# Four rows of expert weights outside the ring instead of two, other pieces for the first and last experts, three transfers and one block of copies moved

## The chip, the core and the metric

The kernel runs on one core of a Trainium2 chip. The metric is the device time of one execution in microseconds (us). Five engines work side by side, each with a queue of its own: TensorE (PE, with weight loads PEld), VectorE (DVE), ScalarE (ACT), GpSimd (POOL) and SyncE (SP), which here issues nearly all DMA transfers. Engines wait for one another through semaphores.

## The reference

```python
def reference(x, ...):                      # x: (1, 256, 1024) float32
    h = x
    p = rmsnorm(h, norm_mix_g) @ w_in       # 8480 columns
    y_conv = short_conv_mixer(...)          # width-3 convolution
    y_rwkv = rwkv7_time_mix(...)            # 16 heads of 64, recurrent state
    h = h + (gate_conv * y_conv + gate_rwkv * y_rwkv) @ w_out
    hn = rmsnorm(h, norm_ffn_g)
    h = h + moe_ffn(hn, router_w, router_b, exp_w1, exp_b1, exp_w2, exp_b2)
    return rmsnorm(h, norm_final_g)

# moe_ffn: 32 experts, 4 of them for each token; for an expert
#   u = x_e @ w1[e] + b1[e]                 # w1[e]: 1024 x 2048 float32, 8 MB
#   y = clamped_swiglu(u) @ w2[e] + b2[e]   # w2[e]: 1024 x 1024 float32, 4 MB
```

## The kernel before

The program has a mixer stage (up to about 386 us in the trace) and an expert stage. The mixer stage takes `w_in` through three buffers in "chunks"; chunk 0 holds the LoRA columns, chunk 1 the first half of the key columns. It ends with the product with `w_out`, the routing and the ranks of the tokens.

**The expert stage** takes all 32 experts one after another. An expert's weights are 12 *rows* of 128 x 2048 float32 (1 MiB each): rows 0 to 7 are `w1`, rows 8 to 11 are `w2`. They lie in `ring`, which has 16 slots of one row. SP issues the loads in the order of use; a load covers 1, 2 or 4 rows, a *piece*. `PARTS` lists the pieces of each kind of expert as (first row, rows), `AT` the slot of its row 0. Before a piece, SP waits in `used` until PE has finished the rows whose slots the piece takes (`w1_used`, `w2_used`). PE waits once for each piece, at the piece's first row, for its whole landing (`row_landed`). So DMA can be at most 16 rows ahead of PE, and the last piece of a slot group decides.

For expert 1, two of its rows (4 and 5) do not lie in the ring but in buffers that are free by then: `side` and the work array `i_SW` (`SIDE`, `load_side`, L496). They let SP load 18 rows before PE has used any: 12 of expert 0, rows 0 to 3 of expert 1, and these two.

PE's work for one expert (`expert`): eight `w1` rows of 8 matmuls each (L1131, `first_rows`); then `between`: the gates of the expert before (`combine`, L1105), the gather of the next expert's tokens (`gather`, L1095), the turn of the activations (L1159), the gates' turn (L1166), the bias of the second product (L1173); then four `w2` rows (L1145, `second_rows`), and the next expert's first bias (L1074). DVE and ACT do SwiGLU meanwhile. The last two experts are interleaved in `last_two` (L1202), with the pieces `w1_30`, `w1_31`, `w2_30`, `w2_31`. `combine` waits for `y_ready`, DVE's copy of the second product out of PSUM (`take_second`, L2173). In the last expert `last_sum` releases the final norm.

**Biases.** `exp_b1` and `exp_b2` are loaded three times each by SP into 96 partitions (L477, L479), behind chunk 2 of `w_in`, and split into three bf16 parts by POOL (L1607 to L1633). POOL first waits for the constants (`const_rest`). At the same time, DVE works on the decays: a scan (L1732) and what follows it, up to the reciprocal (L1747) for which PE waits before L687.

**Final norm.** ACT loads its weights, `gfin`, between its last cast before the expert loop and that loop (L1538). DVE seeds the four PSUM banks of the output with the residual (L2150) after the gates of expert 0, as its last work before the expert loop.

## Time and profile before

| what | value |
| --- | --- |
| median of 3 runs | 1306.29 us (1305.19 to 1309.45) |
| the profiled execution, its own time | 1311.27 us |
| its span, first to last instruction | 1308.7 us |
| PE busy | 1222.7 us, 93% of the span |
| mean granted TensorE clock | 0.981 |
| DMA read | 448.16 MB |
| mean DMA rate over the span | 343 GB/s, about 430 GB/s in the expert stage |
| chain that ended last | PE 67%, DMA 28%, DVE 3% |

The span lies 2.6 us below the profiled execution's own time, and that execution is 5.0 us above the median of the runs: a difference of two versions is worked out on the profiled execution and then taken from the median. In the rows of a timeline the bracket at the end tells how long the engine stood idle ahead of that row, and what released it. All times in rows are us from the start of the span.

### The profile page before, as it was taken

To read this page: it belongs to the slowest core of one execution; us is meant where nothing else is said; L and a number is where in the kernel's file an instruction comes from. 1 tells how busy PE (TensorE), PEld (TensorE's weight loads), DVE (VectorE), ACT (ScalarE), POOL (GpSimd) and SP (SyncE) were. 2 spreads that over 40 slices of the span, in tenths; PEclk is the share of its full clock that TensorE was granted. 3 is DMA by queue.
4 is the path that set the end of the run, shared out by engine and by line. 5 is a ranking of instruction groups with operands and counts; after the bars stand their busy time and mean duration, and the time that the engine had idled before them with its cause. 6 is when DMAs were issued, how large, how long until landed. Compare 5 with 4: busy or idle time off the path is not lost.

```text
span 1308.7 us, 23654 instructions
## 1 busy us (share of the span) xinstructions
PE 1222.7 (93%) x10432; PEld 635.2 (49%) x10433; DVE 310.3 (24%) x615; ACT 213.7 (16%) x345; POOL 57.5 (4%) x32
## 2 busy tenths in 40 slices
PE   8999999999999999998898999899889988998997
PEld 6878888888653343333333333334333333343332
DVE  2473433233151221112111111112111111121112
ACT  4532221311041110001110000011000000011101
POOL 0800120000020000000000000000000000000000
PEclk9999999999989999999999999999999999999999
DMA  9621232246969899999999999999999999999996
GB/s 291 204 72 58 95 104 67 67 131 211 422 260 421 359 433 426 427 430 436 423 433 431 433 423 429 430 431 434 429 428 426 429 431 431 427 432 433 424 431 257
DMA packets 56811, 450.13 MB, mean 344 GB/s; under 512 B 6000, under 2 KB 23920, under 8 KB 35664
## 3 DMA queue, kind: packets, MB, share of 16 engines
q1 hardware_dynamic: 53664, 446.85, 82.6%
q10 hardware_dynamic: 3088, 2.37, 0.6%
q8 instruction: 51, 0.84, 0.3%
q14 instruction: 8, 0.07, 0.0%
HBM read 448.16 MB, written 1.05 MB: 343 GB/s over the span
## 4 chain that ended last, share of the span: by engine, by line
PE 67%; DMA 28%; DVE 3%; issue 1%; ACT 0%; SPq 0%; DVEq 0%; ACTq 0%
DMA ring<-in_exp_w 28%; PE ps L1131 22%; PE sums L635 17%; PE ps L1145 11%; PE sums L1105 3%; PE ps L1095 2%; PE sums L721 2%; PE ps L721 2%; PE sums L1014 1%; PE ps L1014 1%; PE ps L723 1%; PE ps L1159 1%; DVE work L2168 1%; PE ps L1173 1%; PE ps L1074 0%
## 5 line engine op out<-in xcount | busy, mean ns | idle before, releaser
L1131 PE MATMUL ps<-ring,work 128*64 128x512 f32 x2032 | 462.4, 612 | 45.3 <-DMA ring<-in_exp_w 44.5
L1131 PEld LDWEIGHTS ps<-ring,work 128*64 128x64 f32 x2032 | 150.4, 141 | 339.8 <-issue 284.4
L635 PE MATMUL sums<-work,ring 128*128 128x256 f32 (+1 forms) x1120 | 246.0, 386 | 0.6 <-DVE work L1699 0.6
L1145 PE MATMUL ps<-ring,work 128*64 128x512 f32 x992 | 218.3, 592 | 0.0
L635 PEld LDWEIGHTS sums<-work,ring 128*128 128x128 f32 (+1 forms) x1120 | 201.6, 187 | 33.8 <-issue 3.5
L1545 ACT ACTIVATE work<-work 128x512 f32<-128x512 f32 x32 | 20.2, 630 | 725.8 <-DVE work L2156 725.8
L2156 DVE TENSOR_SCALAR work<-ps 128x512 f32<-128x512 f32 x32 | 22.1, 692 | 490.8 <-PE ps L1131 490.8
L1145 PEld LDWEIGHTS ps<-ring,work 128*64 128x64 f32 x992 | 69.6, 136 | 125.8 <-issue 125.6
L2173 DVE COPY work<-ps 128x512 f32<-128x512 f32 x31 | 21.4, 691 | 200.1 <-PE ps L1145 200.1
L1095 PEld LDWEIGHTS ps<-sel,work 128*128 128x128 bf16 x1536 | 53.6, 118 | 24.4 <-issue 24.4
L1105 PE MATMUL sums<-work 64*128 64x512 f32 x248 | 61.6, 615 | 0.0
L1095 PE MATMUL ps<-sel,work 128*128 128x64 bf16 x1536 | 57.1, 198 | 0.0
L1105 PEld LDWEIGHTS sums<-work 64*128 64x128 f32 x248 | 21.3, 186 | 39.8 <-issue 39.8
L1545 ACT ACT_TABLE_LOAD x31 | 39.8, 1283 | 2.1 <-issue 1.5
L1550 ACT ACTIVATE work<-ps 128x512 f32<-128x512 f32 x32 | 19.1, 597 | 68.4 <-PE ps L1095 68.4
L1173 PE MATMUL ps<-work,oh 96*64 96x512 bf16 x64 | 13.0, 403 | 18.1 <-DVE work L2168 18.1
L721 PE MATMUL ps<-ring 64*64 64x64 f32 x960 | 26.8, 220 | 1.7 <-issue 1.7
L721 PEld LDWEIGHTS ps<-ring 64*64 64x64 f32 x960 | 24.5, 135 | 4.4 <-issue 4.4
L2168 DVE COPY work<-ps 128x256 f32<-128x256 f32 x32 | 13.6, 424 | 51.8 <-PE ps L1166 51.8
L1714 DVE SCALAR_TENSOR_TENSOR ring<-sums,par,ring 128x255 f32<-128x255 f32 x24 | 11.5, 478 | 55.9 <-ACT ring L1276 55.6
L1159 PE MATMUL ps<-cst,work 128*128 128x128 f32 x128 | 23.2, 304 | 1.2 <-DVE work L2163 1.2
L721 PEld LDWEIGHTS sums<-ring 64*64 64x64 f32 x640 | 20.4, 135 | 6.1 <-issue 6.1
(282 smaller groups left out, 809.8 us busy)
## 6 DMA issues: line engine op xcount, KB each, us to landing
ring<-in_exp_w SPq DMA_DIRECT2D x103, 2048.0 KB, 30.3
ring<-in_exp_w SPq DMA_DIRECT2D x39, 4096.0 KB, 30.1
ring<-in_exp_w SPq DMA_DIRECT2D x20, 1024.0 KB, 28.5
ring<-in_w_in SPq DMA_DIRECT2D x8, 2048.0 KB, 10.6
ring<-in_w_in SPq DMA_DIRECT2D x16, 1024.0 KB, 7.7
ring<-in_w_out SPq DMA_DIRECT2D x2, 2048.0 KB, 15.8
ring<-in_w_in SPq DMA_DIRECT2D x1, 1152.0 KB, 8.1
work<-in_x SPq DMA_DIRECT2D x2, 512.0 KB, 4.5
```

What stands on the lines that cost most here:

```text
L635: last = mm(bank_of(b)[width * g:width * g + width, 0:T], chunk(n)[:, k, c0:c0 + width], XN[:, k, :], start=k == 0, stop=k == KT - 1)
L721: last = mm(o, a(q, m), b_(q, m), start=True, stop=True)
L1014: last = mm(ps[OUT[t][half]][:, :], Y[:, k, t * P:(t + 1) * P], chunk(NIN + half)[:, k, :], start=k == 0, stop=k == KT - 1)
L1095: last = mm(ps[6][:, k * CAP:(k + 1) * CAP], H3[:, t, s, every_fourth(k)], sel[:, t, :], start=t + s == 0, stop=t + s == 3)
L1105: last = mm(ps[2 * t + half][:, :], gates[64 * half:64 * half + 64, t * P:(t + 1) * P], y[64 * half:64 * half + 64, :], start=False, stop= ...
L1131: last = mm(ps[4 + part][64 * half:64 * half + 64, :], xe[:, k * CAP:(k + 1) * CAP], w[:, part * D + half * 512:part * D + half * 512 + 51 ...
L1145: last = mm(ps[bank][64 * half:64 * half + 64, :], lhs, ring[:, slot(kind, row), a * D + half * 512:a * D + half * 512 + 512], start=False ...
L1159: last = nc.tensor.transpose(ps[4][:, c * P:(c + 1) * P], actb[:, every_fourth(c)], C("ident"))
L1173: last = mm(ps[bank][64 * half:64 * half + 64, :], oh[:, :], b2s[:, half * 512:half * 512 + 512], start=True, stop=False)
L1545: af(sig, glu, ACT.Sigmoid, scale=ALPHA).then_inc(sig_ready, 1)
L2156: ts(glu, ps[4][:, :], LIMIT, None, ALU.min).then_inc(glu_ready, 1)
L2168: cp(dst, ps[bank][:, 0:T]).then_inc(gt_ready, 1)
```

## The change

- `SIDE` gets two more buffers: row 6 of expert 1 goes to `i_XN` and row 7 to `i_CS`. SP loads row 6 once DVE has seeded the output banks, row 7 once the first gather is done and three of POOL's differences are (`h3_left`). Both loads stand behind the load of row 8 of expert 1.
- What lay in `i_CS` moves: `yb` and `actb` to `left0`, `actT` and `gts` to `i_GB`, the last expert's own copies to `i_CS` and `i_GB`; the rows of the final norm go to `i_SW`, its weights to `i_CS`.
- Experts 0 to 3 are written out (`e0` to `e3`), six turns of four experts follow (`TURNS = 6`, was 7), then `e28` and `e29`. All experts from 4 to 29 have the pieces `PLAIN` = (4, 4, 2, 2). Before, the first expert of a turn had pieces of 2, 1, 1, 2, 2, 2, 2 rows and the second of 4, 2, 2, 2, 2.
- Experts 1 to 3 get pieces of one and two rows, and where expert 2's early pieces begin changes: its rows 4 to 7 wait for expert 0's `w2` rows, its rows 8 to 11 for expert 1's first four rows.
- `w1_30` is loaded as 4, 4 (was 2, 1, 1, 2, 2), `w1_31` as 4, 2, 2 (was 4, 4), `w2_30` as 2, 1, 1 (was 2, 2).
- In `last_two` the `combine` of expert 30 stands ahead of the `w2` rows of expert 31, not behind them.
- `exp_b1` is loaded behind chunk 0, ahead of chunk 1; `exp_b2` ahead of chunk 2. POOL waits for the constants only ahead of the router weights' product.
- `gfin` is loaded by ACT after its last work in the expert loop, once the last weights have landed.
- DVE seeds the output banks ahead of the gates of expert 0, and waits for all six bf16 casts of ACT (`h3_cast`) ahead of the expert loop.

```diff
-        TURNS = (E - 4) // 4
-        PARTS = {"e0": ((0, 4), (4, 4), (8, 2), (10, 2)),
-                 "e1": ((0, 2), (2, 2), (6, 1), (7, 1), (8, 2), (10, 2)),
-                 0: ((0, 2), (2, 1), (3, 1), (4, 2), (6, 2), (8, 2), (10, 2)),
-                 1: ((0, 4), (4, 2), (6, 2), (8, 2), (10, 2)),
...
-                 "w1_30": ((0, 2), (2, 1), (3, 1), (4, 2), (6, 2)),
-                 "w1_31": ((0, 4), (4, 4)),
-                 "w2_30": ((8, 2), (10, 2)),
+        TURNS = 6
+        PLAIN = ((0, 4), (4, 4), (8, 2), (10, 2))
+        PARTS = {"e0": PLAIN,
+                 "e1": ((0, 2), (2, 2), (8, 1), (9, 1), (10, 1), (11, 1)),
+                 "e2": ((0, 2), (2, 2), (4, 1), (5, 1), (6, 1), (7, 1), (8, 2), (10, 2)),
+                 "e3": ((0, 1), (1, 1), (2, 2), (4, 2), (6, 2), (8, 2), (10, 2)),
+                 0: PLAIN, 1: PLAIN, 2: PLAIN, 3: PLAIN, "e28": PLAIN, "e29": PLAIN,
+                 "w1_30": ((0, 4), (4, 4)),
+                 "w1_31": ((0, 4), (4, 2), (6, 2)),
+                 "w2_30": ((8, 2), (10, 1), (11, 1)),
...
-        SIDE = {4: side[:], 5: flat(i_SW)}
+        SIDE = {4: side[:], 5: flat(i_SW), 6: flat(i_XN), 7: flat(i_CS)}
...
+            load_second(1, 8, 9)
+            sp.wait_ge(outs_seeded, 2 * TT)
+            load_side(1, 6)
+            sp.wait_ge(gathered, 1)
+            sp.wait_ge(h3_left, 3)
+            load_side(1, 7)
+            load_second(1, 9, 12)
+            load_third(2)
+            load_expert(3, 3, "e3")
...
             # in load_third: where expert 2's pieces wait
+                    used(*((it - 2, last + 4) if last < 8 else (it - 1, last - 8)))
...
                 # last_two
                 second_bias(it + 1, 5)
+                combine(it, gts, yb)
                 pe.wait_ge(at_ready, it + 2)
                 second_rows("w2_31", 8, 12, r, bank=5, turned_act=last_actT)
-                combine(it, gts, yb)
                 combine(it + 1, last_gts, last_yb, last_sum)
...
-            act.wait_ge(h3_cast, 6)
-            act.dma_start(gfin, norm_final_g.partition_broadcast(P)).then_inc(gfin_in, 16)
...
+            act.wait_ge(last_in, n_rounds * 16)
+            act.dma_start(gfin, norm_final_g.partition_broadcast(P)).then_inc(gfin_in, 16)
```

On SP's queue, the start of the program (`in_w_in` 128x8x288 is chunk 0, the next 128x8x512 is chunk 1). Before:

```order
L449 DMA ring<-in_w_in 128x8x288
L455 DMA col<-in_params 32x1 x4
L449 DMA ring<-in_w_in 128x8x512
L466 DMA work<-in_decay_w2 64x1024
...
L474 DMA cst<-in_consts 128x1160
L449 DMA ring<-in_w_in 128x8x512
L477 DMA ring<-in_exp_b1 32x2048 x3
L479 DMA work<-in_exp_b2 32x1024 x3
```

and of the changed kernel:

```order
L453 DMA ring<-in_w_in 128x8x288
L459 DMA col<-in_params 32x1 x4
L462 DMA ring<-in_exp_b1 32x2048 x3
L453 DMA ring<-in_w_in 128x8x512
L472 DMA work<-in_decay_w2 64x1024
...
L480 DMA cst<-in_consts 128x1160
L482 DMA work<-in_exp_b2 32x1024 x3
L453 DMA ring<-in_w_in 128x8x512 x7
```

The three loads of `exp_b1` now stand between chunks 0 and 1, those of `exp_b2` between chunks 1 and 2.

On SP's queue, the loads around the start of the expert stage, from row 5 of expert 1 (`work<-in_exp_w1`) on; 128x2048 is one row, 128x4096 two, 128x8192 four. Before:

```order
L499 DMA work<-in_exp_w1 128x2048
L494 DMA ring<-in_exp_w1 128x2048 x2
L494 DMA ring<-in_exp_w2 128x4096 x2
L494 DMA ring<-in_exp_w1 128x4096
L494 DMA ring<-in_exp_w1 128x2048 x2
L494 DMA ring<-in_exp_w1 128x4096 x2
L494 DMA ring<-in_exp_w2 128x4096 x2
L494 DMA ring<-in_exp_w1 128x8192
L494 DMA ring<-in_exp_w1 128x4096 x2
```

and of the changed kernel:

```order
L502 DMA work<-in_exp_w1 128x2048
L497 DMA ring<-in_exp_w2 128x2048
L502 DMA work<-in_exp_w1 128x2048 x2
L497 DMA ring<-in_exp_w2 128x2048 x3
L497 DMA ring<-in_exp_w1 128x4096 x2
L497 DMA ring<-in_exp_w1 128x2048 x4
L497 DMA ring<-in_exp_w2 128x4096 x2
L497 DMA ring<-in_exp_w1 128x2048 x2
L497 DMA ring<-in_exp_w1 128x4096 x3
```

The 128x8192 row before is the first piece of expert 3; it has become two single rows and a pair. The two `work` rows are the new side rows.

On PE, the end of the expert stage (`ps7` is the second product of expert 30, `ps5` that of expert 31, `sums` the output). Before:

```order
L1145 MATMUL ps7<-ring,work 64x512 x8
L1159 MATMUL ps4<-cst,work 128x128 x4
...
L1173 MATMUL ps5<-work,oh 64x512 x2
...
L1145 MATMUL ps5<-ring,left0 64x512 x8
...
L1105 MATMUL sums0<-work 128x512 x2
L1105 MATMUL sums1<-work 128x512 x2
L1105 MATMUL sums0<-left0,work 128x512 x2
```

and of the changed kernel:

```order
L1165 MATMUL ps7<-ring,work 64x512 x8
L1179 MATMUL ps4<-cst,left0 128x128 x4
...
L1193 MATMUL ps5<-work,oh 64x512 x2
L1125 MATMUL sums0<-left0,work 128x512 x2
L1125 MATMUL sums1<-left0,work 128x512 x2
...
L1165 MATMUL ps5<-ring,work 64x512 x12
...
L1125 MATMUL sums0<-work 128x512 x2
```

The output sums of expert 30 (`left0` holds `yb` now) stand ahead of the `w2` rows of expert 31, so that only those of expert 31 follow them.

## Rows read from the trace of the kernel before

**Rows 1.** The page: GB/s in 40 slices of the span; the chain by engine.
```profile
GB/s 291 204 72 58 95 104 67 67 131 211 422 260 421 359 433 426 427 430 436 423 433 431 433 423 429 430 431 434 429 428 426 429 431 431 427 432 433 424 431 257
PE 67%; DMA 28%; DVE 3%; issue 1%; ACT 0%; SPq 0%; DVEq 0%; ACTq 0%
```

**Rows 2.** Groups by line, PE: tiles, shapes, count, busy us, mean ns, idle before.
```profile
L1131 PE MATMUL ps<-ring,work 128*64 128x512 f32 x2032 | 462.4, 612 | 45.3 <-DMA ring<-in_exp_w 44.5 <-ACT work L1534 0.8
```

**Rows 3.** Stretches: each engine's busy us, PE clock, DMA share, GB/s.
```profile
380.00:390.00 10.00, 8.60 (x35) 5.29 (x38) 8.88 (x29) 4.28 (x6) 4.25 (x2) 0.78 0.51 215
440.00:450.00 10.00, 10.00 (x50) 3.27 (x48) 0.89 (x2) 0.00 (x0) 0.00 (x0) 1.00 0.79 311
460.00:470.00 10.00, 9.41 (x49) 3.28 (x49) 2.08 (x6) 1.96 (x3) 0.00 (x0) 1.00 1.00 424
```

**Rows 4.** Timeline of SP's queue, start of the expert stage: start, length, engine, line.
```profile
390.48 0.33 SPq L494 DMA_DIRECT2D ring<-in_exp_w  x1
...
441.73 0.33 SPq L494 DMA_DIRECT2D ring<-in_exp_w  x1
...
468.16 0.33 SPq L494 DMA_DIRECT2D ring<-in_exp_w  x1
```

**Rows 5.** Timeline of PE, start of the expert stage and late experts.
```profile
434.64 7.04 PE L1145 MATMUL ps<-ring,work 128*64 128x512 f32 x32
...
1109.61 8.55 PE L1131 MATMUL ps<-ring,work 128*64 128x512 f32 x32 [2.55 <-DMA ring<-in_exp_w]
...
1197.55 7.09 PE L1131 MATMUL ps<-ring,work 128*64 128x512 f32 x32 [1.03 <-DMA ring<-in_exp_w]
...
1226.76 7.09 PE L1131 MATMUL ps<-ring,work 128*64 128x512 f32 x32 [2.55 <-DMA ring<-in_exp_w]
...
1246.39 13.90 PE L1131 MATMUL ps<-ring,work 128*64 128x512 f32 x64
```

**Rows 6.** Timeline of PE, then of DVE, last two experts.
```profile
1282.69 3.60 PE L1145 MATMUL ps<-ring,work 128*64 128x512 f32 x16
...
1290.61 7.04 PE L1145 MATMUL ps<-ring,left 128*64 128x512 f32 x32
1297.58 1.99 PE L1105 MATMUL sums<-work 64*128 64x512 f32 x8
...
1290.60 0.69 DVE L2173 COPY work<-ps 128x512 f32<-128x512 f32 x1 [4.88 <-PE ps L1145]
...
1297.69 0.69 DVE L2173 COPY left<-ps 128x512 f32<-128x512 f32 x1 [6.24 <-PE ps L1145]
```

**Rows 7.** Timeline of POOL, DVE and PE, 53 to 74 us.
```profile
53.01 1.03 POOL L1623 CAST work<-work 96x1024 bf16<-96x1024 f32 x1 [0.17 <-POOLq L1620]
54.13 2.13 POOL L1625 TENSOR_TENSOR work<-work 96x1024 f32<-96x1024 f32 x1
56.32 5.05 POOL L1627 CAST work<-work 96x1024 bf16<-96x1024 f32 x1
61.45 2.12 POOL L1629 TENSOR_TENSOR work<-work 32x1024 f32<-32x1024 f32 x1
...
55.07 5.47 DVE L1732 TENSOR_TENSOR_SCAN work<-ring,work 128x2048 f32<-128x2048 f32 x1 [1.24 <-ACT ring L1270]
...
61.55 2.06 DVE L1737 TENSOR_TENSOR dec<-ce,cm 128x24 f32<-128x24 f32 x1
...
73.77 1.15 PE L687 MATMUL ps<-work,side 32*128 32x256 f32 x16 [2.44 <-DVE work L1747]
```

**Rows 8.** Timeline of SP's queue and of PE, first 22 us; then two stretches.
```profile
12.71 7.64 SPq L477 DMA_DIRECT2D ring<-in_exp_b  x3
...
17.22 3.97 PE L635 MATMUL sums<-work,ring 128*128 128x256 f32 x65
...
14.00:17.00 3.00, 3.00 (x15) 2.65 (x14) 1.85 (x2) 0.00 (x0) 0.00 (x0) 1.00 1.10 206
...
28.00:33.00 5.00, 5.00 (x27) 3.99 (x26) 0.48 (x1) 3.32 (x8) 0.00 (x0) 1.00 1.07 185
```

**Rows 9.** The page's DMA issues: KB each, median us to landing; DVE's final norm.
```profile
work<-in_norm_final_g ACTq DMA_DIRECT2D x1, 512.0 KB, 6.0
...
1300.47 1.48 DVE L2214 TENSOR_TENSOR work<-sums,work 128x512 f32<-128x512 f32 x2 [1.98 <-PE sums L1105]
```

More of the change, by code:

```diff
@@ L134, in build @@
         ones_row, scale_diag = left0[:, 0:P], left0[:, P:P + T]
[L135 to L136 removed]
+        gffn, gfin = flat(i_GB)[:, 1024:2048], flat(i_CS)[:, 0:1024]
+        HG = (flat(i_SW)[:, 0:1024], flat(i_SW)[:, 1024:2048])
         par_in = sem("par_in")
@@ L456, in load_in @@
                                          allow_slow_non_contiguous=True).then_inc(mu_in, 16)
+                        for s in range(3):
+                            sp.dma_start(b1f[E * s:E * s + E, :], exp_b1[0]).then_inc(b1_in, 16)
                 else:
@@ L474, in _ @@
                     sp.dma_start(cst[:, P:N_KEPT], consts[:, P:N_KEPT]).then_inc(const_rest, 16)
-                if n == 2:
-                    for s in range(3):
-                        sp.dma_start(b1f[E * s:E * s + E, :], exp_b1[0]).then_inc(b1_in, 16)
                     for s in range(3):
@@ L553, in _ @@
             load_side(1, 5)
-            load_second(1, 1)
-            for u in range(4):
-                load_expert(2 + u, 2 + u, u, u == 0)
-            with sp.Fori(1, TURNS) as i:
-                for u in range(4):
-                    load_expert(i * 4 + (2 + u), i * 4 + (2 + u), u)
+            load_second(1, 8, 9)
[7 more added lines that the diff above has]
+            load_expert(3, 3, "e3")
+            with sp.Fori(0, TURNS) as i:
+                for u in TURN:
+                    load_expert(i * 4 + (4 + u), i * 4 + (4 + u), u)
+            load_expert(28, 28, "e28")
+            load_expert(29, 29, "e29")
             load_last(0)
@@ L1233, in _ @@
                 expert("e1", r * E + 1, r)
+                expert("e2", r * E + 2, r)
+                expert("e3", r * E + 3, r)
                 with pe.Fori(0, TURNS) as i:
-                    for u in range(4):
-                        expert(u, r * E + i * 4 + (2 + u), r, i)
+                    for u in TURN:
+                        expert(u, r * E + i * 4 + (4 + u), r, i)
+                expert("e28", r * E + 28, r)
+                expert("e29", r * E + 29, r)
                 last_two(r * E + (E - 2), r)
@@ L2135, in _ @@
             link(ts(rk[:, :, E:E + 1], rk[:, :, 0:1], -float(CAP), None, ALU.add))
+            v.wait_ge(outs_zeroed, 1)
+            for t in range(TT):
+                for half in range(2):
+                    cp(ps[2 * t + half], HB[:, t, 512 * half:512 * half + 512]).then_inc(outs_seeded, 1)
             v.wait_ge(gates_made, 1)
@@ L2145, in _ @@
             pick_gates(0)
-            v.wait_ge(h3_left, 3)
-            v.wait_ge(outs_zeroed, 1)
-            for t in range(TT):
-                for half in range(2):
-                    cp(ps[2 * t + half], HB[:, t, 512 * half:512 * half + 512]).then_inc(outs_seeded, 1)
+            v.wait_ge(h3_cast, 3 * TT)
             n_rounds = v.value_load(rounds[0:1, 0:1], min_val=1, max_val=4)
```

64 lines of the change are left out of this document (36 added, 28 removed), and 2 rows, old and new, of the table PARTS.

## Prediction

> **What bounds the kernel now.** I read the page first. In its line of GB/s the rate stands at about 430 from the fifteenth slice to the last but one [rows 1]: for 830 us the DMA engines do nothing but bring expert weights, 12 rows of 1.05 MB for each of 32 experts. The chain names PE for 67% and DMA for 28%. The groups by line tell how the two share: PE's `w1` matmuls stood idle 45.3 us, 44.5 of it for weights [rows 2]. The PE timeline shows one expert's rhythm: a pause of 2.55 us ahead of a piece, then 19.6 us of work until the next expert's first row, from 1226.76 to 1246.39 [rows 5]. So from about 570 us on DMA is the bound and PE follows it. Before that, PE runs through and DMA is held by the ring; afterwards the last pause is the one at 1226.76, and from there PE works without a pause to the end, 82 us on the span. **The end is therefore: the landing of the piece that ends PE's last pause, plus PE's own work from there.** Anything that speeds DMA counts as far as that landing; anything that lengthens PE's work behind it counts in full. The mixer stage ahead of it is PE's too, with one pause of size, 2.44 us at 73.77, for DVE [rows 7].
>
> **Bias loads sooner: the gain.** In the timeline from 53 to 74 us POOL splits the second bias while DVE goes through the decays, and the two block each other. POOL's cast took 5.05 us where the same shape took 1.03 just before; it ended when DVE's scan had. DVE's scan was released at 55.07, but POOL's subtraction ran until 56.26, so about 1.2 us of the scan's 5.47 is waiting. DVE's subtraction of 24 elements took 2.06 us and ended together with POOL's next one, 61.45 to 63.57 [rows 7]; for 24 elements nearly all of that is waiting. These two alone are 3.1 us on DVE, and PE's pause that hangs on them is 2.44. In the changed kernel POOL has its data some 20 us sooner and is through before 55 us. I take the whole pause away, −2.4; bounds 0 and −2.4.
>
> **Bias loads sooner: the cost.** `exp_b1` now runs ahead of chunk 1. Its three loads are 0.79 MB, and the stretch in which they ran before moved 185 GB/s [rows 8], so 4.2 us. PE needs chunk 1 at 21.1: its row of 65 matmuls (64 of them the narrow block of chunk 0) ends at 21.19 [rows 8]. Chunk 1 landed in the stretch of 14 to 17 us, where the rate fell to 206 [rows 8]. With 4.2 us on top it lands between 18.2 and 21.2; 0 to 0.1 late from these, and somewhat more where the small LoRA loads share the engines with it. I take +0.5, bounds 0 and +2. Later users (LoRA weights, chunk 2) have at least as much slack. Together the start of the expert stage moves by −1.9.
>
> **Two more side rows and finer pieces.** The reason for them is visible: the rate was 215 GB/s at 380 to 390 and 311 at 440 to 450 [rows 3]. But the ring caps what they can bring. The new loads stand behind the load of row 8 of expert 1, which waits for PE's first row as the load at 390.48 did [rows 4]; the stall around 386 to 391 stays. I let DMA flow again at 391.4, about 0.9 us after that issue (an estimate; both versions have it). From there 18 rows (6 of expert 1, 12 of expert 2) take 18 × 2.43 = 43.8 us, to about 435.2 (2.43 us: 29.21 us for an expert of 12 rows, from 1197.55 to 1226.76 [rows 5]). Expert 3's first row waits for expert 1's first `w2` row, which ends at 434.64 + 1.8 = 436.4 [rows 5]. So DMA stalls again, some 2.4 us with its restart, where the first piece of four waited until 441.73 before [rows 4]. Then comes expert 4's first piece. In both versions it waits for the last row of expert 2, and PE gives that at the same time: issue at 468.16 [rows 4]. Before, DMA still had work then: from the restart at 441.73, 12 + 4 rows = 38.9 us end the piece at 480.6 (plus the same landing lag). In the changed kernel DMA has run dry by then (391.4 + 30 × 2.43 + 3 of stalls = 467.4), and the piece ends at 468.16 + 9.7 = 477.9. **The two extra rows and the fine pieces are worth 2.8 us, not the 4.9 us that two rows take.** After that the cap is 16 rows in both. Bounds: 0 (a new stall behind expert 4) and −4.
>
> **All turns in plain pieces.** A turn of four experts takes 1226.76 − 1109.61 = 117.15 us [rows 5] with the fine pieces, and four plain experts would take 4 × 29.21 = 116.84. Six turns: 6 × 0.31 = −1.9. Landings late in the program are then 2.8 + 1.9 = 4.7 earlier, and 1.9 more with the start: 6.6.
>
> **The tail, first part.** Expert 30's `w1` now comes as 4 + 4 rows. Its second piece lands one expert's loads (10 to 12 rows with 2, 2, 4, 4) behind the one at 1226.76: 29.2 us later. PE reaches its row 4 after 19.63 us [rows 5] plus half of 13.90, 26.6 us. Before, rows 4 and 5 were a piece of their own, landed two rows sooner, and PE had no pause. Now it has one of 29.2 − 26.6 = +2.6 us, and it is the new last pause. Bounds 0 (pieces land faster) and +3.
>
> **The tail, second part.** `combine` of expert 30 now stands ahead of expert 31's `w2` rows. It needs DVE's copy, which ran from 1290.60 to 1291.29, while PE began those rows at 1290.61 [rows 6]; so PE waits 0.7 us. And behind expert 31's rows, the 1.9 us of expert 30's `combine`, which covered the second copy (1297.69 to 1298.38), is gone: PE waits 0.9 us more. Together +1.6, as PE is no longer held by DMA there. If it were, the move would save up to 1.9.
>
> **The rest at nothing.** `gfin` leaves DMA free at 391, within a stretch that the cap at 468.16 covers anyway. At the end it takes up to 6.0 us [rows 9] from the last landing; by the pauses above all weights are in about 8 us ahead of the final norm at 1300.47 [rows 9]. If that cover were gone it would cost about 1. Seeding the banks before the gates delays these by 2.6 us, and PE needs them some 17 us later. The wait for the sixth cast holds DVE's next selection, which PE needs only after the whole of expert 0's `w1`.
>
> **Sum**, on the profiled execution's 1311.27: −2.4 + 0.5 − 2.8 − 1.9 + 2.6 + 1.6 = −2.4, so 1308.9; taken from the median of 1306.29 it is 1303.9.
>
> **A matter of the clock.** After the pause at 1226.76 the piece took 7.09 us, after an equal pause at 1109.61 it took 8.55 [rows 5]: the clock had fallen to half for a while. While PE follows DMA this is free; behind the new last pause 1.5 to 1.7 us of it would be paid. In the plain rhythm a slow piece shortens the next pause to about 1 us (as at 1197.55, which came at full speed), so slow pieces should come at most every second time. The Trainium skill (TensorE: Matmul & The Clock Gate, "HAM oscillation — how this bites in real kernels") describes a loop that waits for DMA and starts every pass at the low clock. By that the pause would always cost, and the time would be 1305.5; the rows show both, so it is a rival.
>
> **The rivals.** *Slow last piece*: as forecast, +1.6: 1305.5. *The ring gives nothing*, because DMA stalls again behind expert 4 or the restart costs more than counted: without the −2.8, 1306.7. For it speaks that two new stalls are certain (436, 468). *The tail costs nothing*: if the last weights set the end, `w1_30`'s pause is absorbed and the moved `combine` is free: 1306.3 − 6.6 = 1299.7. Against it, PE has 26.6 us of work for 29.2 us of loads and then less than DMA brings. *Slower*: the loads of `exp_b1`. Before, SP was held 7.6 us while it issued them [rows 8], since the queue behind chunk 2 was full. If it were held so ahead of chunk 1, that chunk would land at 17 + 4.2 + 6.7 = 27.9, 6.8 late instead of 0.5: 1310.2. It decides from a delay of 2.9 on. Against it, little is queued at 5 us.
>
> **Chances.** Forecast 0.36, slow last piece 0.26, ring gives nothing 0.13, tail costs nothing 0.10, slower 0.07, others 0.08. A measurement of this kernel tells about 0.3%, 3.9 us, from no change. Faster than 1302.4 are the tail's case and a part of the forecast: 0.22. Slower than 1310.2: 0.08. Within: 0.70. The range of 1300 to 1307.5 takes in all but the tail's case and the slow one; the forecast's own with both clocks is 1302.5 to 1306.
>
> **What would show it.** PE's pause at 73.8 should be gone, and no pause over 1 us stand at 21. In SP's timeline, 2.6 to 3.0 us should lie between DMA's end and the issue of expert 4's first piece. Every expert from 4 on should take 29.2 us. The last pause should be ahead of row 4 of expert 30, 2.6 us long. PE should wait 0.7 us ahead of expert 30's `combine`. I am wrong if the last pause is still in expert 29, or if chunk 1 holds PE.

## The result

| | kernel before | changed kernel |
| --- | --- | --- |
| median, 20 runs each, side by side | 1307.38 us | 1309.11 us |
| ratio, 95% interval | | 1.0017 [1.0010, 1.0024] |
| the profiled execution, its own time | 1311.27 us | 1308.43 us |
| its span | 1308.7 us | 1306.8 us |

The change is worth +1.7 us, not the −2.4 that I had worked out. It is within 0.3%, as forecast for the likeliest case, but it lies above the range, and its sign is the other one. One of the 20 executions of the kernel before took 1789.73 us; without it the median is 1307.30, and the ratio is taken without it. The profiled executions point the other way (1306.8 against 1308.7), and that was the first thing to clear up. The kernel before was profiled in an execution 5.0 us above the median of the three runs that I had and 3.9 above that of the 20, the changed kernel in one 0.7 us below its own median.

Lines of the changed kernel are numbered 20 to 24 higher: L1131 is now L1151, L1145 is L1165, L1105 is L1125, L687 is L707, L2173 is L2197. First the page: the rate in 40 slices, and the groups by line of PE (the lines that answer to [rows 1, 2]).

```profile
GB/s 294 202 127 26 110 68 67 99 111 267 421 254 427 390 412 430 436 426 432 431 427 432 429 427 436 431 428 432 433 427 428 432 427 436 432 428 431 432 419 181
L1151 PE MATMUL ps<-ring,work 128*64 128x512 f32 x2016 | 462.4, 614 | 44.9 <-DMA ring<-in_exp_w 44.1
```

PE still stands idle 44.9 us ahead of `w1` rows, where it was 45.3 [rows 2]. The hole that the change aims at has become smaller: the fourteenth slice gives 390 GB/s instead of 359. The last slice gives 181 instead of 257, because the weights end earlier: the last piece has landed 19.9 us before the end of the span, where it was 13.5.

The PE timeline at the places of the prediction: the spot of the old pause at 73.77 [rows 7], then the late experts and the tail (compare [rows 5, 6]).

```profile
70.86 1.15 PE L707 MATMUL ps<-work,side 32*128 32x256 f32 x16
...
1208.76 7.09 PE L1151 MATMUL ps<-ring,work 128*64 128x512 f32 x32 [0.78 <-DMA ring<-in_exp_w]
1218.48 7.09 PE L1151 MATMUL ps<-ring,work 128*64 128x512 f32 x32 [2.63 <-DMA ring<-in_exp_w]
...
1247.68 8.61 PE L1151 MATMUL ps<-ring,work 128*64 128x512 f32 x32 [2.55 <-DMA ring<-in_exp_w]
...
1278.71 3.60 PE L1165 MATMUL ps<-ring,work 128*64 128x512 f32 x16
...
1287.37 1.99 PE L1125 MATMUL sums<-left,work 64*128 64x512 f32 x8 [0.58 <-DVE left L2197]
1289.28 7.09 PE L1165 MATMUL ps<-ring,work 128*64 128x512 f32 x32
1297.16 1.99 PE L1125 MATMUL sums<-work 64*128 64x512 f32 x8 [0.79 <-DVE work L2197]
```

The pause at 74 is gone. A new last pause stands ahead of row 4 of expert 30, at 1247.68, 2.55 us long as forecast, and the piece behind it takes 8.61 us instead of 7.03: the granted clock is at half (the lower of its two levels, 1.2 of 2.4 GHz) from 1247.37 to 1250.78, 3.1 us of this row. PE then waits 0.58 us ahead of expert 30's sums and 0.79 us ahead of expert 31's. From the start of expert 30's `w2` rows at 1278.71 to the last sums at 1297.16 it is 18.45 us; before it was 16.7 (1282.69 to 1299.40).

SP's queue at the start of the expert stage (compare [rows 4]):

```profile
385.06 0.33 SPq L497 DMA_DIRECT2D ring<-in_exp_w  x1
385.44 0.91 SPq L502 DMA_DIRECT2D work<-in_exp_w  x2
...
463.00 0.35 SPq L497 DMA_DIRECT2D ring<-in_exp_w  x1
```

Four stretches of 10 us around it, and four short ones: PE busy, PEld, DVE, ACT, POOL, PE clock, DMA share, GB/s (compare [rows 3]).

```profile
375.00:385.00 10.00, 8.61 (x35) 5.42 (x36) 9.06 (x21) 4.30 (x6) 4.24 (x2) 0.77 0.48 202
385.00:395.00 10.00, 10.00 (x44) 3.10 (x42) 1.51 (x6) 1.73 (x2) 0.00 (x0) 0.89 0.91 351
425.00:435.00 10.00, 9.41 (x90) 4.65 (x88) 3.01 (x7) 2.95 (x4) 0.00 (x0) 1.00 0.88 350
455.00:465.00 10.00, 9.47 (x48) 3.40 (x50) 2.08 (x6) 1.64 (x2) 0.00 (x0) 1.00 1.01 403
...
429.00:433.00 4.00, 3.91 (x20) 1.49 (x22) 0.80 (x4) 1.22 (x1) 0.00 (x0) 1.00 0.72 256
461.00:463.00 2.00, 2.00 (x14) 0.71 (x12) 0.15 (x1) 0.00 (x0) 0.00 (x0) 1.00 0.96 410
463.00:465.00 2.00, 2.00 (x14) 0.70 (x10) 0.74 (x2) 0.00 (x0) 0.00 (x0) 1.00 1.08 320
465.00:467.00 2.00, 2.00 (x12) 0.63 (x10) 0.00 (x0) 0.00 (x0) 0.00 (x0) 1.00 0.69 287
```

The stall ahead of 385 stays (202 GB/s), the stall at 440 has become a smaller one at 430 (256 GB/s from 429 to 433). Expert 4's first piece is issued at 463.00. Expert 0's `w1` starts at 381.35, so that is 81.65 us behind the start; before, it was 468.16 − 386.76 = 81.4 (386.76 is the start of expert 0's first row there). The cap (the wait of expert 4's first piece for a slot of the ring) holds to 0.3 us. The silence of 2.6 to 3.0 us that I had expected between DMA's end and this issue is not there: the piece ahead of it landed at 466.5, 3.5 us behind the issue, and the rate only dipped, to 320 and 287 GB/s from 463 to 467. At 430 GB/s that is 1.2 us lost.

### The profile page after: what moved, and what is told of

It reads as the page before. It is cut to its first block, busy times and chain, and to the rows that moved or that the text cites. A ratio compares the mean times of both kernels' runs of the same rounds, so it can differ in the third digit from the quotient of the medians.

```text
span 1306.8 us, 23554 instructions
## 1 busy us (share of the span) xinstructions
PE 1222.6 (94%) x10432; PEld 629.1 (48%) x10433; DVE 307.3 (24%) x615; ACT 213.8 (16%) x345; POOL 51.6 (4%) x32
## 4 chain that ended last, share of the span: by engine, by line
PE 68%; DMA 29%; DVE 1%; issue 1%; ACT 0%; SPq 0%; DVEq 0%; ACTq 0%
DMA ring<-in_exp_w 28%; PE ps L1151 22%; PE sums L655 18%; PE ps L1165 11%; PE sums L1125 3%; PE ps L1115 2%; PE sums L741 2%; PE ps L741 2%; PE sums L1034 1%; PE ps L1034 1%; PE ps L743 1%; PE ps L1179 1%; DVE work L2192 1%; PE ps L1094 1%; PE ps L1193 1%
## 5 line engine op out<-in xcount | busy, mean ns | idle before, releaser
L1151 PE MATMUL ps<-ring,work 128*64 128x512 f32 x2016 | 462.4, 614 | 44.9 <-DMA ring<-in_exp_w 44.1
L1151 PEld LDWEIGHTS ps<-ring,work 128*64 128x64 f32 x2016 | 144.9, 141 | 343.2 <-issue 272.9
L1165 PE MATMUL ps<-ring,work 128*64 128x512 f32 x1024 | 225.4, 592 | 0.0
L1165 PEld LDWEIGHTS ps<-ring,work 128*64 128x64 f32 x1024 | 71.4, 136 | 130.5 <-issue 130.2
L2197 DVE COPY left<-ps 128x512 f32<-128x512 f32 x31 | 21.4, 692 | 200.1 <-PE ps L1165 200.1
L1125 PE MATMUL sums<-left,work 64*128 64x512 f32 x248 | 61.6, 615 | 0.6 <-DVE left L2197 0.6
L1125 PEld LDWEIGHTS sums<-left,work 64*128 64x128 f32 x248 | 21.3, 186 | 40.2 <-issue 38.9
L1179 PE MATMUL ps<-cst,left 128*128 128x128 f32 x128 | 23.1, 303 | 1.2 <-DVE left L2187 1.2
L741 PE MATMUL sums<-ring 64*64 64x64 f32 x640 | 23.0, 221 | 0.3 <-issue 0.3
## 6 DMA issues: line engine op xcount, KB each, us to landing
ring<-in_exp_w SPq DMA_DIRECT2D x57, 4096.0 KB, 29.2
```

Source lines behind the costliest of these rows:

```text
L741: last = mm(o, a(q, m), b_(q, m), start=True, stop=True)
L1125: last = mm(ps[2 * t + half][:, :], gates[64 * half:64 * half + 64, t * P:(t + 1) * P], y[64 * half:64 * half + 64, :], start=False, stop= ...
L1151: last = mm(ps[4 + part][64 * half:64 * half + 64, :], xe[:, k * CAP:(k + 1) * CAP], w[:, part * D + half * 512:part * D + half * 512 + 51 ...
L1165: last = mm(ps[bank][64 * half:64 * half + 64, :], lhs, ring[:, slot(kind, row), a * D + half * 512:a * D + half * 512 + 512], start=False ...
L1179: last = nc.tensor.transpose(ps[4][:, c * P:(c + 1) * P], actb[:, every_fourth(c)], C("ident"))
```

## The experiments

Each kernel was timed in five rounds against the kernel before, in one series with it. A ratio is to the kernel before of the same series (1306.62, 1306.89, 1306.86 and 1306.64 us). "Start" is the start of expert 0's first `w1` row in the kernel's own profiled execution; times "behind the start" are counted from it, which takes the mixer stage out.

Two kernels of one series, with 11 or 12 executions each (b_w30 has 8), can be compared to about ±1.5 us (95%, from drawing the executions anew). The ratio and the difference of the medians are taken in different ways and differ by up to 0.9 us.

### Taking single parts into the kernel before

**b_again**: the kernel before, no edit.

> The kernel before, unchanged, profiled a second time. Theory A (the first profile was typical): PE starts expert 0 at 386.8 us as before, with the pause of 2.4 us for DVE near 73.8, span about 1308.7; then the changed kernel, whose span is 1306.8, cannot be slower than before by a gain that is only in the mixer stage. Theory B (the first profile caught a long execution; its own time of 1311.27 is 3.9 above the median of 20 runs): expert 0 starts at 382 to 385, and the span is about 1305; the shorter mixer stage then is not a gain of the change. Time ratio 1.000 by both.

1308.10 us, 1.0013 [1.0003, 1.0023]. The same program built again differs by 1.5 us. Its pause at 74 was there, 2.77 us long; its start was at 384.96, 1.8 sooner than in the execution that I had predicted from. A difference of 1 to 2 us from a single build of this kernel is therefore weak evidence.

**b_bias**: both bias loads sooner, and the wait for the constants later.

```diff
+                        for s in range(3):
+                            sp.dma_start(b1f[E * s:E * s + E, :], exp_b1[0]).then_inc(b1_in, 16)
...
-                if n == 2:
-                    for s in range(3):
-                        sp.dma_start(b1f[E * s:E * s + E, :], exp_b1[0]).then_inc(b1_in, 16)
...
-            pool.wait_ge(const_rest, 32)
...
+            pool.wait_ge(const_rest, 32)
```

The loads of `exp_b1` now stand behind chunk 0, those of `exp_b2` ahead of chunk 2 (the cut lines no longer hold them back to `n == 2`), and the wait behind the splitting of the biases.

> The kernel before with one part of the change alone: the first bias is loaded ahead of chunk 1, the second ahead of chunk 2, and POOL waits for the constants only ahead of the router weights' product. By the first pair of profiles this part brought expert 0 forward by 5.4 us, so theory A says 4 to 5.4 us faster. Theory B says 0 to 2 us faster, as the pause and the lower clock behind it are not in most executions of before. Were the delay of chunk 1 larger in most runs than in the profiled one, it would be slower.

1306.06 us, 1.0002 [0.9993, 1.0012]. The pause at 74 is gone (the row at 70.92 has no wait), and the start is at 382.67. Against the kernel before of the series the medians give −0.6 and the ratio +0.3, against b_again the medians give −2.0. The pause goes as forecast; what that is worth is not known to better than this.

**b_comb**: only `combine` of expert 30 moved ahead.

```diff
+                combine(it, gts, yb)
                 pe.wait_ge(at_ready, it + 2)
                 second_rows("w2_31", 8, 12, r, bank=5, turned_act=last_actT)
-                combine(it, gts, yb)
```

> The kernel before with the sums of expert 30 ahead of expert 31's second product, and nothing else. If PE is the bound at the end, PE waits 0.7 us ahead of those sums and 0.9 more ahead of the last ones: slower by 1.6 us. If the last landing is the bound (it is 2.4 us ahead of the end of PE's last row before), the move saves up to 1.9 us; with a delay of 2.6 us for expert 31's rows they are not held by DMA, so I expect +1.6.

1309.63 us, 1.0026 [1.0013, 1.0038]: +3.0, or +1.5 against b_again. Its PE timeline shows both waits that I had put at 0.7 and 0.9:

```profile
1288.70 1.99 PE L1105 MATMUL sums<-work 64*128 64x512 f32 x8 [0.57 <-DVE work L2173]
1290.62 7.09 PE L1145 MATMUL ps<-ring,left 128*64 128x512 f32 x32
1298.50 1.99 PE L1105 MATMUL sums<-left,work 64*128 64x512 f32 x8 [0.79 <-DVE left L2173]
```

**b_w30**: only the last rows of `w1_30` as one piece.

```diff
-                 "w1_30": ((0, 2), (2, 1), (3, 1), (4, 2), (6, 2)),
+                 "w1_30": ((0, 2), (2, 1), (3, 1), (4, 4)),
```

> The kernel before with rows 4 to 7 of expert 30 in one piece of four and not in two of two, and nothing else. Theory of the tail: PE then waits about 2.5 us ahead of row 4 of expert 30, slower by 2.5 us, by 4.0 to 4.2 if the clock falls there. Rival: PE's slack behind it takes the pause up, no change.

1310.93 us, 1.0033 [1.0020, 1.0045] (8 runs): +4.3, or +2.8 against b_again. The pause comes, and in this trace the slow clock with it:

```profile
1241.84 7.03 PE L1131 MATMUL ps<-ring,work 128*64 128x512 f32 x32
1251.57 8.70 PE L1131 MATMUL ps<-ring,work 128*64 128x512 f32 x32 [2.69 <-DMA ring<-in_exp_w]
```

As many matmuls of the same kind take 7.03 us ahead of the pause and 8.70 behind it: 2.69 + 1.67 = 4.4 us in this execution.

### Taking single parts out of the changed kernel

**a_again**: the changed kernel, no edit.

> The changed kernel, unchanged, once more. The same kernel before gave 1308.1 against 1306.6 when it was built and loaded a second time (ratio 1.0013). If a build and load has an offset of its own of about 1.5 us, this one lies within 1.5 us of 1309.1 in time, and its profile gives expert 0 a start of 381 to 383, the last pause of 2.5 to 2.7 us ahead of row 4 of expert 30, with a slow clock behind it in most executions.

1308.08 us, 1.0011 [0.9996, 1.0025]. Its last two pauses:

```profile
1219.68 8.78 PE L1151 MATMUL ps<-ring,work 128*64 128x512 f32 x32 [2.54 <-DMA ring<-in_exp_w]
...
1248.90 7.09 PE L1151 MATMUL ps<-ring,work 128*64 128x512 f32 x32 [0.86 <-DMA ring<-in_exp_w]
```

Here the slow stretch fell behind the pause before the last. That made PE later by 1.7 us and the last pause shorter (0.86) by as much, and the row behind it ran at full speed. The two landings are 29.22 us apart, as the prediction said. So from the last pause to the end of the span it is 57.5 us here, and 59.1 in the first build of the changed kernel (1247.68 to 1306.8). Which of the two an execution gets is the 1.6 us of the rival "slow last piece".

**a_fine30**: expert 30's second piece in two.

```diff
-                 "w1_30": ((0, 4), (4, 4)),
+                 "w1_30": ((0, 4), (4, 2), (6, 2)),
```

> The changed kernel with rows 4 to 7 of expert 30 in two pieces of two again. Theory of the tail: the pause of 2.6 us ahead of row 4 and the slow clock behind it (1.5) go, the last pause is in expert 29 again; the clock may fall there at no cost. 2.6 to 4.1 faster than the changed kernel. Rival: DMA ends so close behind that PE waits at a later piece instead, gain under 1 us.

1304.99 us, 0.9983 [0.9972, 0.9994], −3.1 against a_again. The last pause is now in expert 29, and expert 30 runs through:

```profile
1219.87 8.78 PE L1151 MATMUL ps<-ring,work 128*64 128x512 f32 x32 [2.56 <-DMA ring<-in_exp_w]
...
1241.20 13.90 PE L1151 MATMUL ps<-ring,work 128*64 128x512 f32 x64
```

**a_comb**: `combine` of expert 30 back behind expert 31's rows.

```diff
-                combine(it, gts, yb)
                 pe.wait_ge(at_ready, it + 2)
                 second_rows("w2_31", 8, 12, r, bank=5, turned_act=last_actT)
+                combine(it, gts, yb)
```

> The changed kernel with the sums of expert 30 behind expert 31's second product again. With PE the bound at the end: 1.6 to 1.8 us faster than the changed kernel (its own profile has a wait of 0.58 ahead of these sums and of 0.79 ahead of the last ones). Rival, DMA the bound: no gain.

1306.37 us, 0.9993 [0.9981, 1.0005], −1.7 against a_again; b_comb says the same with the other sign. In the timeline both waits are gone:

```profile
1285.95 7.04 PE L1165 MATMUL ps<-ring,work 128*64 128x512 f32 x32
1292.92 1.99 PE L1125 MATMUL sums<-left,work 64*128 64x512 f32 x8
1294.74 1.88 PE L1125 MATMUL sums<-work 64*128 64x512 f32 x8
```

**a_bias**: both bias loads back behind chunk 2, and POOL waits for the constants first again. (The `exp_b2` loop is not in the cut: it stands right behind the added lines and falls under `if n == 2` with them.)

```diff
-                        for s in range(3):
-                            sp.dma_start(b1f[E * s:E * s + E, :], exp_b1[0]).then_inc(b1_in, 16)
...
+                if n == 2:
+                    for s in range(3):
+                        sp.dma_start(b1f[E * s:E * s + E, :], exp_b1[0]).then_inc(b1_in, 16)
...
+            pool.wait_ge(const_rest, 32)
```

> The changed kernel with both bias loads where they were, and POOL's wait for the constants too. Profiles of four executions with the old order have expert 0 start at 383.5 to 386.8 (mean 385.0), two with the new at 381.4 and 382.7. So 3 us slower than the changed kernel, start of expert 0 at 383.5 to 387, a pause of 0.5 to 2.8 us near 74. Rival: the mixer stage varies by itself and the order is worth nothing, same time.

1310.21 us, 1.0019 [1.0006, 1.0032], +2.1 against a_again by the medians and +1.0 by the ratios. The time says that the sooner loads are worth 1 to 2 us, but the profiled execution doesn't show how: there is no pause at 74 in it.

```profile
72.96 1.15 PE L708 MATMUL ps<-work,side 32*128 32x256 f32 x16
```

The two engines did meet in it: a POOL copy of 5.05 us (57.27) lay beside DVE's scan. But DVE's reciprocal, for which this row waits, was done at 71.81, and PE came only at 72.96. Its start is at 384.48, later than in any profiled execution with the new order of loads, and the 2 us are there already at this row (72.96 against 70.86). Yet the twelve traces with the new order have this row at 70.55 to 73.13, none with a wait, so the trace of a_bias doesn't tell where the +2.1 comes from.

### Putting the parts together

**a_both**: a_fine30 and a_comb together.

> The changed kernel with both parts of the tail undone: expert 30's rows 4 to 7 in two pieces, its sums behind expert 31's second product. One alone gave 1305.0 (3.1 faster than the changed kernel's second build at 1308.1), the other 1306.4 (1.7 faster). If they are two separate costs on PE's path they add: 1303.3. If DMA takes over as the bound once one is gone, the second brings nothing: 1305.

1302.83 us, 0.9974 [0.9960, 0.9987], 4.0 us faster than the kernel before and 5.2 faster than the second build of the changed one (each against the kernel before of its series, −4.0 and +1.2). The two parts add up (−3.1 and −1.7 make −4.8). From the last pause of expert 29 to the end it is 82.8 us, as in the kernel before (81.9, the prediction's 82) plus a wait of 0.67 for expert 30's first piece. A part of this kernel's gain is not the tail's: its landings came 1.5 us sooner than in a_again (835.8 against 837.3 us behind the start); the section on the landings says why.

**a_heads**: experts 0 to 5 written out, six turns for experts 6 to 29, none written out behind the turns but the last two.

```diff
-        HEADS, TURN = ("e0", "e1", "e2", "e3"), (0, 1, 2, 3)
-        TAIL = ("e28", "e29", "w1_30", "w1_31", "w2_30", "w2_31")
+        HEADS, TURN = ("e0", "e1", "e2", "e3", "e4", "e5"), (0, 1, 2, 3)
+        TAIL = ("w1_30", "w1_31", "w2_30", "w2_31")
```

> The changed kernel with experts 0 to 5 written out and six turns of four for experts 6 to 29, in place of 28 and 29 written out behind the turns. In the changed kernel an instruction fetch goes over one of the 16 DMA engines as PE reaches expert 28, and the next landing comes 1.07 late (10.78 for 9.71) and stays late, as the weights of an expert land with their slowest engine. Theory: with no new code behind the turns, all landings from there on are 1.0 to 1.1 earlier, 1 us faster, 1307. Rival: the fetch falls elsewhere at the same price, no gain.

1310.07 us, 1.0025 [1.0013, 1.0036], +3.2 and so no faster than any build of the changed kernel. My theory was that the instruction fetches of the written-out experts 28 and 29 delay the landings late in the program, and that moving them to the front would free these. It fell: the fetches moved to the front, 13 of them by 649 us and none from there to the last pause, and the landings were as late (the second piece of expert 29 landed 837.0 us behind the start, 837.1 in the changed kernel). The section on the landings takes that up.

**a_best**: a_both and a_heads together.

> Both parts of the tail undone and experts 0 to 5 written out. If all three add: 1308.1 less 3.1, 1.7 and 1.0, so 1302.3, and faster than the kernel before by 4.

1304.24 us, 0.9974 [0.9957, 0.9992]: the same ratio as a_both, 1.4 us slower by the medians. The third part did not add; whether experts are written out at the front or at the end makes no difference that these runs can tell.

**a_e4**: a_best, with expert 4's first piece in three.

```diff
-                 0: PLAIN, 1: PLAIN, 2: PLAIN, 3: PLAIN, "e4": PLAIN, "e5": PLAIN,
+                 0: PLAIN, 1: PLAIN, 2: PLAIN, 3: PLAIN, "e4": ((0, 1), (1, 1), (2, 2), (4, 4), (8, 2), (10, 2)), "e5": PLAIN,
```

> As the one before it, and expert 4's first piece of four rows as 1, 1 and 2. The theory that the ring of 16 rows caps what the side rows bring: expert 4's first piece waits for the last row of expert 2 and DMA runs dry ahead of it for about 2 us. With single rows it can start 5.2 us sooner (three rows of 1.72), and all landings behind it come 1.5 to 2 us earlier: 1300.5. Rival: the stall is not there or only moves to expert 5's first piece, same time as the one before it.

1302.56 us, 0.9971 [0.9960, 0.9982]. The bytes of expert 4's first piece were in 92.8 us behind the start, 1.2 sooner than in a_best (94.0). The forecast was 1300.5 us; the time doesn't tell it from a_best or a_both. The stall at the cap can be made smaller by finer pieces, by about 1 us of landing in this one trace; its profiled span of 1297.3 is the shortest of all, but it is that of an execution 3.4 us below its median.

### Side rows, and what a build is worth

**a_lateside**: the two new side rows are issued later, when PE has finished expert 0's `w1` rows and the rest of expert 1 has been issued.

```diff
+            load_second(1, 9, 12)
+            used(0, 7)
             sp.wait_ge(outs_seeded, 2 * TT)
             load_side(1, 6)
             sp.wait_ge(gathered, 1)
             sp.wait_ge(h3_left, 3)
             load_side(1, 7)
-            load_second(1, 9, 12)
```

> The changed kernel, but the two new side rows (rows 6 and 7 of expert 1) are issued only after rows 9 to 11 of expert 1, and after PE has finished all eight w1 rows of expert 0, about 14 us later than in the changed kernel. They then bring DMA nothing ahead of the ring's cap. Theory of the cap: the landings of the late experts are set by expert 4's first piece, which PE releases about 81.6 us after the start of expert 0 in both kernels, so the time is that of the changed kernel within 0.5 us, and row 52 (expert 4's first piece) lands 94 us after the start. Rival, the extra rows themselves are what the landings gained: everything behind lands 2.9 us or more later and the time is about 3 us longer.

1308.54 us, 1.0009 [0.9994, 1.0023]: that of the changed kernel (a_third, of the same series, 1308.63). Its SP queue, the side rows (x2) and then expert 4's first piece:

```profile
400.17 1.37 SPq L502 DMA_DIRECT2D work<-in_exp_w  x2
...
464.94 0.36 SPq L497 DMA_DIRECT2D ring<-in_exp_w  x1
```

Two stretches of it, of the same columns as above:

```profile
387.00:397.00 10.00, 10.00 (x46) 3.13 (x44) 1.55 (x6) 1.76 (x2) 0.00 (x0) 0.90 0.86 310
397.00:407.00 10.00, 8.22 (x84) 4.15 (x82) 3.85 (x8) 3.11 (x4) 0.00 (x0) 1.00 0.86 337
```

And those of a_third:

```profile
387.00:397.00 10.00, 10.00 (x42) 3.14 (x40) 1.94 (x7) 2.19 (x2) 0.00 (x0) 0.86 0.86 339
397.00:407.00 10.00, 8.22 (x82) 4.19 (x80) 3.86 (x8) 3.11 (x4) 0.00 (x0) 1.00 1.03 433
```

The side rows are issued 16.8 us behind the start instead of 4.1 (400.17 and 387.90), 12.7 later. DMA loses (339 − 310 + 433 − 337) × 10 us = 1.25 MB, 2.9 us at 430 GB/s. Counted behind the start, row 24 came at 24.0 instead of 20.6 us, 3.4 later, and row 52, the end of expert 4's first piece, at 94.2 against 94.5. The delay is gone there: the cap has eaten it. **Bringing the side rows early is worth nothing by itself.** That leaves the finer pieces of experts 1 to 3 and their earlier waits for what the ring's start gains. It is a conclusion by exclusion: no kernel was run with the finer pieces and without the two rows.

**a_both2**, **b_third**, **a_third**: a_both, the kernel before and the changed kernel, built once more.

> The same program as a_both, built again: the changed kernel with w1_30 as 4, 2, 2 and the combine of expert 30 back behind expert 31's w2 rows. If the 4 us by which a_both was faster than the kernel before are real, this build is 3.5 to 5.5 us faster too. If a build alone can move the time by such an amount, it comes out elsewhere, by up to 1.5 us by what two builds of the kernel before differed.

1304.70 us, 0.9984 [0.9974, 0.9994]. Faster again, by 1.9 instead of 4.0. In its profiled execution the second piece of expert 29 landed 837.9 us behind the start, in a_both's 835.8.

> The kernel before, built a third time. The second build was 1.0013 of the first. If the difference belongs to builds, this one lies between 0.999 and 1.0015; the two theories of the tail don't enter.

1306.82 us, 0.9998 [0.9987, 1.0010].

> The changed kernel, built a third time. The first build was 1.0017 of the kernel before, the second 1.0011. My sum after the experiments is +0.4 us (1.0003). If the rest is the build's, this one may lie between 0.999 and 1.0025; if it is the change's, it is again 1.0010 to 1.0017.

1308.63 us, 1.0014 [1.0005, 1.0024].

The three builds of the changed kernel gave 1.0017, 1.0011 (its interval takes in 1) and 1.0014, the two further builds of the kernel before 1.0013 and 0.9998. The changed kernel is slower in every build, by 1.2 to 2.0 us. A build of its own moves a kernel by up to 2 us (b_again, a_both2), so the sign of the change is likely, and its size is known to about 1 us.

## Why the prediction was wrong

**The step that failed** is the size of the sum's terms, and the largest is that of the sooner landings. I put them at −4.7 us (−2.8 for the ring, −1.9 for the turns) and took it that a landing moves with the bytes. They came 2.4 us sooner. The mechanism of the other terms was right: the pause at 74 went, the last pause moved to expert 30 and the moved `combine` cost what it should. But the start gave −1.4 instead of −1.9, and expert 30's pause cost +3.1 instead of +2.6, as the slow clock behind it was left out of the sum. A gain of 2.4 us became a loss of 1.7, also because the time I subtracted from was 1.1 us low.

With three profiled executions of either kernel, their parts can be averaged. "Landing" is the end of the pause ahead of row 4 of expert 29, behind the start; "rest" is what follows up to the end of the span.

| | start | landing | rest | span |
| --- | --- | --- | --- | --- |
| before | 386.76 | 840.0 | 81.9 | 1308.7 |
| b_again | 384.96 | 839.9 | 82.0 | 1306.9 |
| b_third | 383.61 | 840.2 | 81.9 | 1305.7 |
| changed | 381.35 | 837.1 | 88.3 | 1306.8 |
| a_again | 382.39 | 837.3 | 86.7 | 1306.4 |
| a_third | 383.81 | 838.4 | 86.7 | 1308.9 |
| difference of the means | −2.6 | −2.4 | +5.3 | +0.3 |

**The baseline.** I took the sum from 1311.27 to 1308.9 and the difference from a median of three. The time of the kernel before came out as 1307.38 in 20 runs: 1.1 of the 5.2 us between 1303.9 and 1309.11 are this. The other 4.1 are the sum.

**The start: right in kind, −1.4 instead of −1.9.** The pause at 74 went in every trace with the new order. Chunk 1 landed at 19.7 instead of 16.9 us, within the bounds worked out, and didn't hold PE at 21; SP issued the three loads of `exp_b1` in 1.5 us instead of 7.6. So the +0.5 was not needed there and the rival by `exp_b1` fell. Behind it the slack was not as large as I took it: PE waited 0.47 us at 38.1 (a_fine30) and 0.66 us at 38.2 (a_both2) for a chunk of `w_in`, and in no trace with the old order.

But the step "I take the whole pause away, −2.4" took one execution for all. The pause was 2.44, 2.77 and 2.47 us in the three of the kernel before, 0.51 in b_comb and 0.84 in b_w30, whose programs are the same up to there, and none in a_bias. This row starts at 73.2 us on the mean of the six traces with the old order and at 71.5 on that of the twelve with the new. The timed pairs give −0.6 (b_bias), −2.0 (b_bias against b_again) and −2.1 (a_bias); I take −1.4, the middle. The −2.6 of the table is larger because all three executions of the kernel before were above their medians (by 3.9, 0.8 and 0.7 us; those of the changed one by −0.7, 0.0 and 2.0). Corrected by these means (1.8 and 0.4), the profiled times differ by −0.2 + 1.4 = +1.2 us, in line with the timings. All 18 traces give the same −2.6 for the start (384.7 and 382.1), and −1.3 when the same correction is made (their executions lay 1.1 above and 0.2 below their medians).

**The ring: right, −2.9 against −2.8.** By the bytes, row 96 came in 204.1 us behind the start before and 201.5 in the changed kernel (204.3 and 201.1 in the second builds, 204.5 and 201.6 in the third). The cap argument holds: SP's issue at 81.65, and a_lateside, which shows that two rows sooner or later ahead of the cap change nothing. My picture of DMA there was too dark in both places: 256 GB/s for 4 us, 1.6 us lost, where I had a stall of 2.4 us, and 1.2 us lost at the cap where I had it run dry. That the total still fits is in part luck. The rival "the ring gives nothing" was not the cause.

**The turns: −1.1 instead of −1.9.** From row 96 to row 360 (22 experts) the bytes took 644.0 us in all traces with the old pieces and 642.9 in the changed kernel. The step "a turn takes 117.15 and four plain experts 116.84" was the difference of two single intervals, each read to 0.1 us or so, times six.

**The landings: +1.6 that I didn't have.** By the bytes the late rows are 4.0 us sooner (−2.9 − 1.1), by the landings 2.4. A piece has landed when the slowest of its 16 parts has. Between the first and the last part of a piece lay 2.0 to 2.2 us in the three traces of the kernel before, from about 530 us to expert 29. In the changed kernel it was 3.6, 4.3 and 4.8 us by expert 29 in its three traces. The steps came right behind instruction fetches: in the first trace 2.5 until a fetch at 1204, then 3.6, and that piece landed 10.8 us behind the one ahead of it instead of 9.7; in a_third 3.3 until a fetch at 1209, then 4.8; in a_again 2.5 until a fetch at 580, then 4.2; in a_both2 3.0 until one at 578, then 4.5. A fetch brings 16 KB and takes 0.9 to 1.1 us. The DMA summary of the kernel before, from 395 us to the pause in expert 29 (queue, kind, packets, MB, share of the engines):

```profile
q1 hardware_dynamic: 20342, 354.02, 99.8%
...
q8 instruction: 8, 0.13, 0.1%
```

And that of the changed kernel:

```profile
q1 hardware_dynamic: 17302, 352.01, 100.1%
...
q8 instruction: 12, 0.20, 0.1%
```

Eight fetches were there before, twelve are now: the changed kernel writes out more experts (two at the front would have been in the loop, two behind it). PE waits for the last part, and once the spread had grown in a stage with DMA fully busy, it did not shrink again. But not every fetch makes a step, and their number doesn't set the lag: a_bias and a_both had 12 fetches too, and spreads of only 2.0 and 2.5 us at expert 29, where their pieces landed 834.3 and 835.8 us behind the start. a_both and a_again show the lag alone: their bytes came at the same times (row 360 at 844.1 in both), the spreads were 2.5 and 4.3, and the landings 835.8 and 837.3. So the lag differs between executions or builds of nearly the same program; which of the two, no run tells. That the fetches cause it is inferred from the times at which it grows. a_heads moved them to the front (13 ahead of this piece), and the lag was 3.6 us all the same; a kernel of this kind with fewer fetches was not run, so the cause stays open.

**Expert 30's pause: +3.1 (a_fine30 against a_again) instead of +2.6.** Place and length were right (2.55; the landings 29.2 apart), and "the last pause should be ahead of row 4 of expert 30" held in all eight traces of kernels whose `w1_30` ends in a piece of four. The term left out the clock, although I had seen it. In five of these eight (changed, b_w30, a_comb, a_bias, a_heads) the row behind the last pause was a slow one, 8.6 to 8.8 us. In the three others it took 7.09, behind a pause of about 0.85 twice (a_again, a_third) and of 2.55 once (a_lateside). So the rival "slow last piece" was not a rival but a part of the forecast that comes in some executions: 59.1 to 59.3 us from the last pause to the end in the changed kernel, a_bias and a_heads, 57.5 to 57.7 in a_again, a_third and a_lateside. The Trainium skill (TensorE: Matmul & The Clock Gate, "HAM oscillation — how this bites in real kernels") has the loop start each pass at the low clock. That loop waits for DMA some 3 to 5 us in each pass, longer than the 2.55 us here, and the traces agree with it only in part: some passes start at the low clock and others at the full one, the last one slow five times in eight.

**The moved `combine`: +1.7 instead of +1.6.** The waits were 0.58 and 0.79, the stretch 1.7 us longer, and a_comb gave it back (−1.7; −2.1 between a_fine30 and a_both).

**The terms at nothing: right as far as the traces show.** `gfin` landed at 1290.6, ahead of the final norm at 1298.3. PE's wait for DVE in the first expert, 1.20 us, is the same in both kernels.

**Sum** with the sizes that were measured: −1.4 − 2.4 + 3.1 + 1.7 = +1.0, where three builds gave +1.7, +1.2 and +2.0. Of the 4.1 us by which the sum was off, 2.3 are the landings (turns and lag, less the ring's 0.1), 0.5 the start, 0.5 the clock and 0.1 the combine; the last 0.7 are less than a build moves the time.

**The range** failed for a reason of its own. Each rival was priced alone, and I stopped at 1307.5. "Ring gives nothing" with "slow last piece" would have been 1308.3, and neither excluded the other. Three of the sizes that I had chosen lay at the good end of their bounds: the whole pause, the whole difference of the turns, no slow clock. And the median of three from which I subtracted was 1.1 us low.

## What to carry to other kernels

Where PE follows DMA, a sooner landing pays only up to the last pause, and a coarser last piece can give it all back. The two edits in the tail cost 4.8 us, more than the 3.8 that the edits ahead of it gained (1.4 at the start, 2.4 by the landings); with both undone the rest of the change is worth 2 to 4 us (a_both, a_both2, a_best and a_e4). Before rows are added outside a ring, ask which wait caps the ring behind them: bringing the two side rows early was worth nothing, and the 2.9 us must come from the finer pieces. Behind DMA, count the landing of a piece's last part and not its bytes. And do not build a sum of 2 us on one profiled execution of a kernel whose identical builds differ by 1.5.

## What the hardware showed that I had not expected

- The profile counts instruction fetches (16 KB, 0.9 to 1.1 us each) among the packets of the 16 DMA engines that bring the weights. At 100% DMA the spread between the 16 parts of a piece grew right behind some of them, by 1.1 (changed kernel, 1204) to 1.7 us (a_again, 580), and did not shrink again for 600 us. Behind others it stayed.
- The half clock at a pause of 2.55 us lasted 3.4 us (changed kernel, 1247.37 to 1250.78) and cost 1.6. Behind equal pauses of 2.55 us it came in some cases and not in others: at 1249.79 of a_lateside the row took 7.09 us, at 1247.68 of the changed kernel 8.61.
- The start of the expert stage of one and the same program varied from 383.61 to 386.76 us in three builds, 3.15 us, as much as the largest single effect of the change.
